# A mixture-of-experts decoder step on one core: the down-projection weight transfers begun from ScalarE's queue instead of SyncE's

## What is computed

```python
def expert_block(args):
    toks, e = args
    gu = x[toks] @ w_gate_up[e] + b_gate_up[e]          # (1024, 2048) weights
    g = jnp.minimum(gu[:, :D_FF], SWIGLU_LIMIT)
    u = jnp.clip(gu[:, D_FF:], -SWIGLU_LIMIT, SWIGLU_LIMIT)
    act = (u + 1.0) * (g * jax.nn.sigmoid(SWIGLU_ALPHA * g))
    return act @ w_down[e] + b_down[e]                  # (1024, 1024) weights
```

## Time and profile before

| | |
|---|---|
| Median of 3 runs | 1567.96 us |
| Profiled execution | 1569.08 us, span 1567.2 us |
| TensorE busy | 1440.4 us, 92% |
| VectorE, ScalarE busy | 459.3 us, 241.1 us |
| Queue q1 (SyncE's) | 475.01 MB |
| Queue q10 (ScalarE's) | 2.60 MB |

### The profile page before, as it was taken

The page is one execution under the profiler, slowest core; times in us unless marked ns, Lnnn a source line. Parts: engine busy times, 40 slices in busy tenths (PEclk is TensorE's granted clock), DMA queues, the critical chain, the costliest instruction groups (busy, mean ns, idle before and its releaser), DMA issues.

```text
span 1567.2 us, 16621 instructions
## 1 busy us (share of the span) xinstructions
PE 1440.4 (92%) x6659; PEld 584.5 (37%) x6659; DVE 459.3 (29%) x977; ACT 241.1 (15%) x436; POOL 79.9 (5%) x71
## 2 busy tenths in 40 slices
PE   3899999997799968999999999999999999999994
PEld 0464555564343442333333333333333333333321
DVE  2324587763212131212122122122122122122124
ACT  1011232113300122111111111111111111111111
POOL 0200420131000020000000000000000000000000
PEclk7899999999899967999999999999999999999997
DMA  9233226236573714999999999999999999999991
GB/s 351 71 108 119 91 98 161 98 124 220 211 277 129 287 45 174 431 428 428 427 428 428 428 428 429 429 428 429 428 428 428 428 429 428 429 429 429 428 429 54
DMA packets 74268, 488.68 MB, mean 312 GB/s; under 512 B 6217, under 2 KB 16777, under 8 KB 48625
## 3 DMA queue, kind: packets, MB, share of 16 engines
q1 hardware_dynamic: 71488, 475.01, 74.3%
q0 software_dynamic: 1792, 10.49, 1.9%
q10 hardware_dynamic: 946, 2.60, 0.5%
HBM read 483.96 MB, written 4.08 MB: 311 GB/s over the span
## 4 chain that ended last, share of the span: by engine, by line
DMA 41%; PE 27%; DVE 2%; ACT 1%; issue 1%; POOL 0%; POOLq 0%; DVEq 0%; SPq 0%; ACTq 0%
DMA ring<-in_w_gate_up 41%; PE ps L1413 12%; PE ps L1448 3%; PE ps L881 2%; PE ps L882 2%; PE ps L885 1%; PE ps L1360 1%; PE ps L1391 1%; PE ps L1307 1%; PE ps L1324 1%; PE ps L1406 1%; PE ps L1348 0%; PE ps L1330 0%; PE ps L1432 0%; POOL z L542 0%
## 5 line engine op out<-in xcount | busy, mean ns | idle before, releaser
L1413 PE MATMUL ps<-ring,z 128*64 128x512 f32 x2048 | 452.7, 596 | 24.2 <-DMA ring<-in_w_gate_up 24.2
L1413 PEld LDWEIGHTS ps<-ring,z 128*64 128x64 f32 x2048 | 142.0, 137 | 333.4 <-issue 276.2
L1448 PE MATMUL ps<-ring,z 128*64 128x512 f32 x1024 | 226.0, 594 | 0.4 <-ACT z L797 0.4
L1968 DVE TENSOR_SCALAR actT<-ps 128x512 f32<-128x512 f32 x32 | 22.1, 692 | 659.8 <-PE ps L1413 659.8
L1448 PEld LDWEIGHTS ps<-ring,z 128*64 128x64 f32 x1024 | 72.0, 137 | 148.9 <-issue 143.8
L898 PE MATMUL ps<-ring,actT 128*128 128x512 f32 (+1 forms) x208 | 106.4, 593 | 0.5 <-ACT actT L577 0.5
L899 PE MATMUL ps<-ring,actT 128*128 128x512 f32 (+1 forms) x208 | 104.3, 583 | 0.0
L1360 PE MATMUL ps<-z,actT 128*64 128x512 f32 x384 | 90.9, 610 | 0.2 <-DVE actT L1930 0.2
L1391 PE MATMUL ps<-z,aT 128*128 128x512 f32 x128 | 67.4, 630 | 1.7 <-ACT z L803 1.2
L1951 DVE TENSOR_TENSOR z<-z,ps 128x512 f32<-128x512 f32 x64 | 44.0, 688 | 62.9 <-PE ps L1391 62.9
L793 ACT ACTIVATE actT<-actT 128x512 f32<-128x512 f32 x32 | 20.1, 627 | 262.9 <-DVE actT L1968 262.9
(11 more groups left out here) (310 smaller groups left out, 1306.0 us busy)
## 6 DMA issues: line engine op xcount, KB each, us to landing
ring<-in_w_gate_up SPq DMA_DIRECT2D x128, 2048.0 KB, 23.7
ring<-in_w_down SPq DMA_DIRECT2D x64, 2048.0 KB, 20.6
ring<-in_w_ada SPq DMA_DIRECT2D x12, 2048.0 KB, 9.2
ring<-in_w_in SPq DMA_DIRECT2D x12, 2048.0 KB, 7.9
ring<-in_w_branch_b SPq DMA_DIRECT2D x2, 2048.0 KB, 10.6
ring<-in_w_out SPq DMA_DIRECT2D x2, 2048.0 KB, 10.8
ring<-in_state SPq DMA_DIRECT2D x8, 256.0 KB, 7.7
ret_sample<-ring SPq DMA_DIRECT2D x8, 256.0 KB, 5.7
```

The lines of the kernel that those rows point to most:

```text
L1413: done = nc.tensor.matmul(bank(q // 2)[64 * (q % 2):64 * (q % 2) + 64, :], lhs, ring3[k // 2][:, (k % 2) * 2048 + q * BANK:(k % 2) * 2048 ...
L1448: done = nc.tensor.matmul(bank(2)[64 * q:64 * q + 64, :], lhs, ring3[4 + k // 4][:, (k % 4) * D + q * BANK:(k % 4) * D + (q + 1) * BANK], ...
```

## The change

The loop of SyncE starts only the four gate-up chunks of the experts 1 to 31. The two down chunks of the next expert are started by ScalarE, in its `expert`, between the copy of the next rows and the wait for the last down matmul. Expert 0's down chunks, and those of the second pass (`base` not 0), stay with SyncE.

```diff
+        def down_rows(e, k):
+            r = (k - 4) * 512
+            return a["w_down"][bass.ds(e, 1), r:r + 512, :].rearrange("a (p i) n -> (a p) (i n)", i=4)
...
             with sp.Fori(1, NE) as e:
-                for k in range(6):
+                for k in range(4):
                     sp.wait_ge(chunk_used, e * 6 + (k - 5))
                     chunk(e, k)
...
-            def expert(p, half, buf, first, last):
+            def expert(p, half, buf, first, last, base):
...
                 if not last:
                     xt_out(n + 1)
+                if base == 0 and not last:
+                    for k in range(4, 6):
+                        act.wait_ge(chunk_used, n * 6 + (k + 1))
+                        act.dma_start(ring3[k], down_rows(n + 1, k)).then_inc(chunk_here[k], 16)
                 act.wait_ge(chunk_used, n * 6 + 6)
                 y = ysb[buf][64 * half:64 * half + 64]
```

More of the change, by code:

```diff
@@ L410, in chunk @@
                         "a (p i) n -> (a p) (i n)", i=2)).then_inc(chunk_here[k], 16)
-                r = (k - 4) * 512
-                return sp.dma_start(ring3[k], a["w_down"][bass.ds(e, 1), r:r + 512, :].rearrange(
-                    "a (p i) n -> (a p) (i n)", i=4)).then_inc(chunk_here[k], 16)
+                return sp.dma_start(ring3[k], down_rows(e, k)).then_inc(chunk_here[k], 16)
             for k in range(4):
@@ L803, in expert, with pair @@
                 nc.scalar.activation(y[:, 512:D], bank(2)[NS:P], ACT.Copy).then_inc(y_done, 1)
-            def pair(p, buf, first, last):
-                expert(p, 0, buf, first, False)
-                expert(p, 1, buf, first, last)
+            def pair(p, buf, first, last, base):
+                expert(p, 0, buf, first, False, base)
+                expert(p, 1, buf, first, last, base)
             def sum_out(t, banks):
@@ L823, in experts @@
                 p0, pairs = base // 2, count // 2
-                pair(p0, 0, True, False)
+                pair(p0, 0, True, False, base)
                 with act.Fori(0, (pairs - 2) // 2) as i:
-                    pair(i * 2 + (p0 + 1), 1, False, False)
-                    pair(i * 2 + (p0 + 2), 0, False, False)
-                pair(p0 + pairs - 1, 1, False, True)
+                    pair(i * 2 + (p0 + 1), 1, False, False, base)
+                    pair(i * 2 + (p0 + 2), 0, False, False, base)
+                pair(p0 + pairs - 1, 1, False, True, base)
                 gather_out(p0 + pairs - 1)
```

## The result

The changed kernel took 1575.36 us (median of 6 runs, 1573.33 to 1575.86) against 1567.63 us for the kernel before in the same comparison: ratio 1.0048, 95% interval 1.0034 to 1.0062, so 5 to 10 us slower. The forecast was 1576. One of the six runs of the kernel before took 3020.85 us; without it their median is 1567.31 us. The profiled execution has a span of 1573.6 us, 6.4 us more than before.

The account below looks back on a forecast made before the run. Transfers, through G3's landing, were taken as the bound after TensorE's early lead. The profiled 1569.08 + 0 + 0 + 7.9 + 0 = 1577.0 us; that execution stood 1.1 us above the median, so 1576 us, range 1564 to 1594 (8 in 10).

Parts of the forecast that it names:

- The bound: Expert stage: TensorE needs 28.15 us an expert, transfers 29.37; the lead is used up, then G3's landing sets the time.
- SyncE and ScalarE cost 0: Issuing engines: SyncE's two fewer issues and waits, and ScalarE's two added issues ahead of the result's copies, cost 0.
- Equal shares: Transfer engines: the two queues get equal shares while both have work; likeliest case, with variants +4.9 to +9.8 us, chance 0.55.
- The term, +7.9 us paid once: Ahead of G3's landing: 15.8 us at half rate serve 7.9 us of down chunks formerly behind it, paid once.
- The total: Whole kernel: 1576 us, 0.5% slower, which is within what a comparison calls the same.
- Rate unchanged with two queues: Sharing stretches, two thirds of each expert: rate stays 428 GB/s, cost 0; each 1% of rate would be 6.0 us.
- Landings: Issue to landing: gate-up median 18 us instead of 23.7, down chunks median 15 us instead of 20.6.
- First wait: Expert stage: TensorE begins to wait for G3 six experts sooner, near 720 us instead of near 900 us.
- Idle time: Gate-up matmuls: TensorE's idle time grows from 24.2 to about 32 us.
- order unchanged: Rival, queues: SyncE's served first or down chunks wait anyway, so G3 keeps its lead; +0, 1568 us, chance 0.08.
- a loss and a gain of rate: Rivals, sharing stretches: loss up to 3.9% (1578 to 1599 us) 0.19, above it 0.07; gain (1552 us at most) 0.11.

Follow-up runs that it names:

- the halved chunks: Kernel before and changed kernel, each loading only the first half of every down chunk of experts 1 to 31: 1537.03 and 1537.27 us.
- the first experiment: All six chunks of experts 1 to 31 issued by ScalarE in one queue, against the kernel before: 1567.68 against 1568.45 us, ratio 0.9996.

## Why the prediction was right, point by point

- **The bound** (TensorE early on, the transfers later): right. What it is worth was set too low: "at most the waits, 24 us", against 31 us with the halved chunks, some 29 of them in the stage. A wait also breaks the row of matmuls: 48 and 16 of them are busy 10.52 + 3.65 = 14.17 us, 64 in a row 13.95 us. That is 0.22 us at each of the 25 waits, 5.5 us beside the 24.2.
- **SyncE and ScalarE cost 0**: right, shown by the first experiment (six issues of ScalarE's an expert, −0.8 us) and by the halved chunks (+0.2 us). The copies of the result start about 0.5 us later than before, one issue, as said. The cover is that their readers come late: the only wait of TensorE for them, 1.2 us at the very end, is as long in both kernels.
- **Equal shares**: right, 2.20 and 2.13 MB side by side, and the same time with the queues swapped.
- **The term, +7.9 us paid once**: right in mechanism, 1.6 us too large; the stage shows 6.3. The step that failed took the sharing from the *issue* of D0 at +13.6 to the *landing* of G3 at +29.4. A transfer's bytes begin to move after its issue and end before its landing; with the lone transfer's 2.9 us for both it is (15.8 − 2.9) / 2 = 6.4 us. With the same correction D1 alone was forecast at +4.5 and measured at +4.2. The count of bytes says the same without a replay: 2.65 MB, 6.2 us, ahead of each G3. It also shows that the 2.9 us stand for more than they say: in the middle of the stage the second queue moves nothing for over 3 us after D0's issue alone, and has 2.65 of the 5.16 MB behind that, a little over half.
- **The total.** 1576 was said and 1575.36 measured, 0.6 us apart, where the term was off by 1.6. That the one is smaller than the other is luck: the medians differ by 7.7 us, with an interval of 5 to 10.
- **Rate unchanged with two queues**: right, 428 GB/s in all three stretches. The 367 and 418 GB/s of the earlier trace rows, which carried the range's ends, came from a stretch with small loads; the range was wider than it had to be.
- **Landings**: gate-up median 17.8 (18 said), down 14.9 (15 said). One by one, in the middle expert, the fit is looser: G0 to G3 16.3, 17.8, 20.4 and 25.5 us where 14.6, 16, 20.4 and 25.6 were said, D0 13.9 and D1 20.3 us where 13 to 18 were. So the agreement of the medians is in part luck.
- **First wait**: six experts sooner, near 720 us, was said. In the timelines it is at 706 us, where the kernel before has it at 817; that is four experts. The 720 us were counted back from a first wait "near 900 us", which the kernel before doesn't have: two errors that partly cancel.

```profile
817.38 3.65 PE L1413 MATMUL ps<-ring,z 128*64 128x512 f32 x16 [0.29 <-DMA ring<-in_w_gate_up]
```
```profile
706.08 3.65 PE L1419 MATMUL ps<-ring,z 128*64 128x512 f32 x16 [1.28 <-DMA ring<-in_w_gate_up]
```
- **Idle time** at the gate-up matmuls: 28.1 us, where 32 was said; the kernel before has 24.2. The same matmuls are also busy 2.4 us longer (455.1 against 452.7), 1.7 us of it in 16 of them at a lower clock (last section). Idle and busy together grew by 6.3 us, as the stage did.
- **The rivals**: order unchanged is out by the landings, a loss and a gain of rate by the 428 GB/s.

## What to carry to other kernels

Where one queue already keeps the transfers without a gap, it hands them over in the order of need; a second queue adds no bytes per second, it only changes the order, and puts what is needed later beside what is needed next. The time from issue to landing, which fell by a quarter here, says nothing on whether the right transfer lands in time. Count what is served ahead of the transfer that is waited for; it was paid once where the queues never ran dry and nothing else was late, and in nearly every round in the run where a down chunk came late. Two queues with pieces of unequal size don't share by bytes: here the one with the short pieces got a fifth.

## What the runs showed of the hardware

A wait of TensorE can cost clock, but its length alone doesn't say whether it does. In the changed kernel one wait for G3 was 2.29 us long; the 16 matmuls behind it took 5.35 us instead of 3.65, and from 942.2 to 945.4 us the clock was at 0.50, the lower of its two levels (1.2 and 2.4 GHz):

```profile
941.64 5.35 PE L1419 MATMUL ps<-ring,z 128*64 128x512 f32 x16 [2.29 <-DMA ring<-in_w_gate_up]
```
```profile
942.20:945.40 3.20, 3.20 (x10) 0.88 (x8) 0.00 (x0) 0.00 (x0) 0.00 (x0) 0.50 1.01 430
```

Three other runs have one such wait each, with the same 5.35 us behind it: 2.10 us with the changed order, 2.20 us with one down chunk in the second queue, 2.28 us with the queues swapped. Waits of 1.07 us had no such effect. But in the run with the later issue 28 of the 30 waits were 2.02 to 2.69 us long, and the 16 matmuls behind each of them took 3.65 us, at full clock; one of them:

```profile
1065.50 3.65 PE L1454 MATMUL ps<-ring,z 128*64 128x512 f32 x16 [2.59 <-DMA ring<-in_w_down]
```

Only the other two, of 3.92 and 3.17 us, were followed by slow matmuls (5.28 and 5.35 us). What decides at 2 to 3 us, these runs don't show.

Where it happened in the changed kernel, at 941.64 us, the lower clock cost nothing, since the transfers set the beat: from the wait at 882.29 us to that at 1029.16 us there are five experts of 29.37 us, with this one among them. In the tail it costs time: the kernel with one down chunk in the second queue ran its last expert at full clock, the changed kernel didn't, in the same window (PEclk is the last but two):

```profile
1522.00:1547.00 25.00, 20.44 (x81) 6.52 (x77) 7.39 (x11) 2.85 (x5) 0.00 (x0) 1.00 0.26 111
```
```profile
1522.00:1547.00 25.00, 21.86 (x87) 7.00 (x83) 4.65 (x7) 1.96 (x4) 0.00 (x0) 0.93 0.33 141
```

From the last G3's start to the end of the span they took 1568.3 − 1524.9 = 43.4 and 45.1 us. The order in one queue had 43.5 us too. These 1.6 us are most of the difference between stage and median (2.1 us) with one down chunk in the second queue, and half of it (3.2 us) with the changed order. The tail's instructions are the same in all of these kernels; that the clock falls in one execution and not in the next is an effect as large as a fifth of the change measured here.
